# Forget-gate attention scores: two rounded passes over all 128 rows per head, in place of native fp32 over 64 rows

## The chip, the cores and the metric

The kernel runs on one core of one Trainium2 chip. The metric is the device time of one execution in microseconds (us). Engines are named as in the profile: PE is the matrix engine TensorE, PEld its weight loads, DVE is VectorE, ACT is ScalarE, SP issues transfers.

## The reference, cut to what matters

The program is two transformer layers and a third block over 512 tokens of width 1024. The change touches one place, the mixer of the second layer, attention with a forget gate, 16 heads of 64 channels (the function is cut):

```python
def _fox_attend(q, k, v, log_f):
    c = jnp.cumsum(log_f, axis=1)
    ...
        s = jnp.einsum('bqhd,bkhd->bhqk', q_b, k, preferred_element_type=jnp.float32) * (d ** -0.5)
        s = s + cq_b[..., :, None] - ck[:, :, None, :]
        s = jnp.where(kpos[None, :] <= qpos[:, None], s, NEG_INF)
        w = jax.nn.softmax(s, axis=-1).astype(v.dtype)
        return jnp.einsum('bhqk,bkhd->bqhd', w, v)
```

It runs for four blocks of 128 queries. Block number qb sees the keys of blocks 0 to qb, so its scores are 128, 256, 384 or 512 columns wide. `q`, `k` and `v` are projections of the layer's input.

## The kernel before

Every projection splits both operands into a rounded part (type fp32r, tiles with H) and the rest (tiles with L), and adds three products: high by high, low by high, high by low (L400, L401, L402 in `lin_parts`). A weight tile arrives by DMA in RAW, ACT rounds it to WH (`hi_ahead`, L364), DVE subtracts to get WL (`lo_ahead`, `lo_one`, L370), both three tiles ahead of use. ACT, DVE and PE each run a list that is fixed in the program and strictly in order; semaphores tie the lists together.

The forget-gate stage takes the 16 heads as 8 pairs. The two heads of a pair sit in one tile, one in rows 0 to 63, the other in rows 64 to 127. A pair is four steps, one per query block qb. In each step c of `pe_attend` PE issues

1. the scores of the next step (`pe_scores`, L483, native fp32; PE executes each such product as two records, so a step has four), and then the mask, a bf16 product per head added to the same bank (L491),
2. at qb = 0 the product of weights and values of the pair before (L529),
3. the transposes of this step's probabilities (L502),
4. `project_ahead`: six times three products (L400 to L402), a quarter of the 72 products that project queries (part 0), keys (part 1) and values (part 2) of the next pair. A part is eight times three products. Part 0 ends in the second call of step qb = 1, part 1 in the fourth call of step qb = 2; two more calls follow in that step, and then come the scores of the next pair's block 0, which need that pair's queries and keys.

ACT in a step copies the transposes out (L616) and computes the exponentials of the next step (L592); then in `project_ahead` it rounds one weight tile (L364) and copies one finished part out of its PSUM bank: QF (L2354) after qb = 1, KF (L2356) after qb = 2, VT (L2360) after qb = 3. DVE in a step adds the decay rows BC to the next step's scores and takes the row bound (L572), normalises (L605, L607), and then in `project_ahead` calls `skip()`, which subtracts one weight tile (L370) and does nothing else. The parts alternate between two PSUM banks; PE starts a part when the semaphore `evac` of its bank says that the one before was read.

ACC, 16 KB in each partition, isn't used during this stage.

Of the kernel before, what the change touches and what calls it, by code (L numbers as in the profile page):

```python
# [16 lines left out]
F32, F32R, BF16, I32 = mybir.dt.float32, mybir.dt.float32r, mybir.dt.bfloat16, mybir.dt.int32  # L17
ALU, ACT, AX = mybir.AluOpType, mybir.ActivationFunctionType, mybir.AxisListType
P = 128
T = 512  # L20
# [51 lines left out]
class Counts:  # L72
# [17 lines left out]
 ptev pv o_hi o_lo sinkexp bandv sum7 sum8 mean cen sqr var ln_t x_new h_relu h_sq h_hi h_lo fl fox_c chain_d  # L90
 chain_a chain_p out_t gate_t gate_s pt_hi pt_lo kept mem_in tabb_in sq2 rn r_hi r_lo pooled pw_in y_hi y_lo ix ixr ixs
 topk hsp hg_x hg_prod hg_read hg_e hg_d hg_o hg_small hx mn m2 varb ln_v x_full sum7q pj pj_free memsum cross xsum
 asum ysum h_up quad mvt yt yo ot_in xt_in z r_tok merge os brf var_out var_in""".split()


def program(nc, known, t):

    cnt = Counts(known)
    ctx = ExitStack()
    with ctx:  # L100
        sem = {n: ctx.enter_context(nc.semaphore(n)) for n in SEMS}
# [6 lines left out]
        evac = [ctx.enter_context(nc.semaphore(f"evac{b}")) for b in range(2)]  # L108
        PB = [ctx.enter_context(nc.psum_tensor(f"PB{i}", [P, T], F32)) for i in range(8)]
# [4 lines left out]
        def at(name, shape, dt, off):  # L114
            return nc.alloc_sbuf_tensor_at(name, shape, dt, offset=off)

        def sb(name, shape, dt):
            size = (int(np.prod(shape[1:])) * (2 if dt == BF16 else 4) + 31) // 32 * 32
            h = at(name, shape, dt, top[0])
            top[0] += size  # L120
            return h
# [8 lines left out]
        acc_at = top[0]  # L130
# [15 lines left out]
        def region(name, shape, dt):  # L146
            return sb(name, shape, dt)
# [7 lines left out]
        VT = region("VT", [P, T], F32)  # L155
# [40 lines left out]
        top[0] = mixer  # L196
        OH = region("OH", [P, DT, T], F32R)
        OL = region("OL", [P, DT, T], F32R)
        QF = region("QF", [P, 2, T], F32)
        KF = region("KF", [P, 2, T], F32)  # L200
        BC = region("BC", [P, 2, 2, T], F32)
        VP = region("VP", [P, 2, TT, P], F32)
        FZ = region("FZ", [16, 5, T], F32)
# [119 lines left out]
        def wait(eng, name, key):  # L323

            eng.wait_ge(sem[name], cnt.value(name, key))

        def done(ins, name, key):

            ins.then_inc(sem[name], 1)
            cnt.note(name, key)  # L330
# [13 lines left out]
        def evac_of(eng, m):  # L344

            eng.wait_ge(evac[m % 2], m // 2 + 1)
# [19 lines left out]
        def lo_one(eng, n):  # L366

            s, nb = n % 4, blocks_of(n)
            eng.wait_ge(hi_done[s], n // 4 + 1)
            eng.tensor_tensor(WL[:, s, 0:nb], RAW[:, s, 0:nb], WH[:, s, 0:nb].bitcast(F32), ALU.subtract).then_inc(lo_done[s], 1)  # L370

        def lo_ahead(dve, st, k=0, i=0, per=0):

            if per == 0:
                if st.n + k + 3 < total_tiles:
                    lo_one(dve, st.n + k + 3)
                return
            s, u = st.slot(k + 3, i, per)
            dve.wait_ge(hi_done[s], u + 1)
            dve.tensor_tensor(WL[:, s], RAW[:, s], WH[:, s].bitcast(F32), ALU.subtract).then_inc(lo_done[s], 1)  # L380
# [38 lines left out]
        def keys(kind, qb):  # L419

            return {"swa": list(range(max(qb - 1, 0), qb + 1)), "mem": [0, 1]}.get(kind, list(range(qb + 1)))
# [9 lines left out]
        def operands(kind, h):  # L431
            r = slice(h % 2 * 64, h % 2 * 64 + 64)
            if kind == "mla":
                return QM[:, h], KM[:, h], lambda j: V4[:, j, h * 64:h * 64 + 64]
            if kind == "swa":
                return QS[r, h // 2], K2[r, h // 4], lambda j: VS[:, j, h // 4 * 64:h // 4 * 64 + 64]
            if kind == "fox":
                pp = h // 2 % 2
                return QF[r, pp], KF[r, pp], lambda j: VP[:, pp, j, h % 2 * 64:h % 2 * 64 + 64]
            if kind == "dsa":  # L440
                return SQ_[r, h // 2], SK2[r], lambda j: SV[:, j]
            return MQ[r, h // 2], MK[r, h // 2], lambda j: MV[:, j, h * 64:h * 64 + 64]

        def item(kind, h, qb):

            return ((HEAD0[kind] + h) // 2 * 4 + qb) * 2 + h % 2
# [4 lines left out]
        def score_read(n):  # L451

            return "biased" if n // 8 in BIASED else "score_free"
# [5 lines left out]
        def pe_scores(pe, kind, g, qb):  # L459

            ns = [item(kind, 2 * g + e, qb) for e in range(2)]
            ks = keys(kind, qb)
            lo = (ks[0] - qb + 1) * P if kind == "swa" else 0
            w = len(ks) * P
            plain = kind in ("swa", "mem")
            xs = [None, None]
            for e in range(2):
                if ns[e] >= 2:
                    wait(pe, score_read(ns[e] - 2), ns[e] - 2)
            if kind == "fox" and qb == 0:  # L470
                evac_of(pe, M_FOX + 3 * g)
                evac_of(pe, M_FOX + 3 * g + 1)
            if kind == "swa" and qb == 0:
                evac_of(pe, M_A["q", g])
            if kind == "mla" and qb == 0:
                evac_of(pe, M_A["uq", 2 * g])
                evac_of(pe, M_A["uq", 2 * g + 1])
                evac_of(pe, M_A["ukv", 2 * g])
                evac_of(pe, M_A["ukv", 2 * g + 1])
                pe.wait_ge(sem["chain_a"], cnt.value("chain_a", "krope"))  # L480
            for e in range(2):
                q, k, _ = operands(kind, 2 * g + e)
                xs[e] = pe.matmul(PB[2 + e][:, lo:lo + w], q[:, qb * P:qb * P + P], k[:, ks[0] * P:ks[0] * P + w], start=True, stop=plain)  # L483
                if plain:
                    done(xs[e], "scores", ns[e])
            if not plain:
                for e in range(2):
                    if kind == "dsa":
                        x = pe.matmul(PB[2 + e][:, 0:w], ID16[:], MSK[:, qb, 0:w], start=False, stop=True)
                    else:  # L490
                        x = pe.matmul(PB[2 + e][:, w - P:w], ID16[:], CA16[:], start=False, stop=True)  # L491
                    done(x, "scores", ns[e])
# [391 lines left out]
        M_FOX = M_IN + 101  # L884
# [986 lines left out]
        def _(act):  # L1871
            st = Stream()
# [25 lines left out]
            def step():  # L1898
                hi_ahead(act, st)
                lin_ready(act, st)  # L1900

            def nxt():
                st.n += 1
                st.m += 1
# [444 lines left out]
            def project(j, part):  # L2349
                pp = j % 2  # L2350
                step()
                b, ub = st.bank(0)
                if part == 0:
                    x = act.activation(QF[:, pp], PB[b][:], ACT.Copy, scale=-0.125)  # L2354
                elif part == 1:
                    x = act.activation(KF[:, pp], PB[b][:], ACT.Copy)  # L2356
                else:
                    if j:
                        act.wait_ge(sem["misc"], cnt.value("misc", ("vp", j - 1)))
                    x = act.activation(VT[:], PB[b][:], ACT.Copy)  # L2360
                x.then_inc(evac[b], 1)
                nxt()
            for part in range(3):
                project(0, part)

            def project_ahead(c):
                j, qb = divmod(c, TT)
                if j < 7 and qb:
                    project(j + 1, qb - 1)
# [12 lines left out]
        def _(dve):  # L2382
            st = Stream()
# [24 lines left out]
            def nxt():  # L2408
                st.n += 1
                st.m += 1  # L2410

            def skip():
                lo_ahead(dve, st)
                nxt()
# [19 lines left out]
            def token_major(key, dst):  # L2434
                dve.wait_ge(sem["misc"], cnt.value("misc", key))
                done(dve.tensor_copy(dst, PB[7][:].rearrange("p (j n) -> p j n", n=P)), "misc_free", key)
# [722 lines left out]
            b, ub = st.bank(0)  # L3159
# [7 lines left out]
            done(dve.memset(FZ[:, 0], 1.0), "chain_d", "fone")  # L3167
            dve.wait_ge(sem["chain_d"], cnt.value("chain_d", "fone"))
            done(dve.tensor_tensor_scan(FZ[:, 3], FZ[:, 0], FZ[:, 2], 0.0, ALU.mult, ALU.add), "fox_c", 0)
            for part in range(3):  # L3170
                skip()
            token_major(("vp", 0), VP[:, 0])

            def project_ahead(c):
                j, qb = divmod(c, TT)
                if qb:
                    if j < 7:
                        skip()
                elif j:
                    token_major(("vp", j), VP[:, j % 2])  # L3180
            dve_attend(dve, ("fox",), 8, project_ahead)
            p_low(1)

# [43 lines left out]
```

## Time and profile before

| | |
|---|---|
| runs of the program | 2237.23, 2237.76, 2239.43 us; median 2237.76 |
| profiled execution, first to last instruction | 2236.6 us (the page shows no other time of it) |
| PE, PEld busy | 2182.0 us (98%), 1726.4 us (77%) |
| DVE, ACT, POOL busy | 1254.3 us (56%), 908.3 us (41%), 230.7 us (10%) |
| chain that ended last | PE 86%, DVE 8%, issue 3%, ACT 3% |
| forget-gate stage, first to last scores | 680.4 to 869.6 us |
| period of a pair | 25.37 us (725.60 to 750.97 us) |

The durations of matrix products overlap, since they are pipelined: what one costs is the distance between two starts. Before two products in a row the weights of the second are loaded under the first, where nothing hinders it. The busy times of PE count time spent in flight; they don't say that the engine is at its peak.

### The profile page before, as it was taken

The numbers are of one execution on the slowest core, as the hardware profiler recorded it, in microseconds if no ns is written. First come the engines' busy times: TensorE is split into PE (matmuls) and PEld (weight loads), VectorE is DVE, ScalarE is ACT, GpSimd is POOL, SyncE is SP. The second block draws the span as 40 slices with busy tenths as digits, with TensorE's granted clock in tenths as the row PEclk, the third lists the DMA queues.
The fourth block names the chain that finished last, engine by engine and source line by source line (L and its number), as shares of the span: only waits on it lengthen the run. The fifth ranks groups of instructions, "written<-read, shape, count | busy, mean of one in ns | idle before, by whom it ended". The sixth has DMA issues, their size and how long they took to land.

```text
span 2236.6 us, 27997 instructions
## 1 busy us (share of the span) xinstructions
PE 2182.0 (98%) x10187; PEld 1726.4 (77%) x10189; DVE 1254.3 (56%) x1993; ACT 908.3 (41%) x1502; POOL 230.7 (10%) x151
## 2 busy tenths in 40 slices
PE   7999999999999999999999999999999999999998
PEld 5767788888777777788888777678778787888886
DVE  5676643343474554643243377388589678544454
ACT  3565433233254544443243264433543444222333
POOL 0000400001400001400001320133000230000001
PEclk9999999999999999999999999999999999999999
DMA  6113233333223331333333244124222232323322
GB/s 173 27 45 102 74 98 104 86 102 103 76 77 100 98 95 48 94 94 106 92 94 103 78 112 110 56 72 113 73 66 66 75 105 76 103 76 113 94 68 73
DMA packets 368307, 196.92 MB, mean 88 GB/s; under 512 B 21040, under 2 KB 362813, under 8 KB 368206
## 3 DMA queue, kind: packets, MB, share of 16 engines
q1 hardware_dynamic: 367794, 195.51, 30.6%
q8 instruction: 63, 1.03, 0.2%
q14 instruction: 38, 0.31, 0.0%
q10 hardware_dynamic: 412, 0.07, 0.0%
HBM read 193.40 MB, written 2.14 MB: 87 GB/s over the span
## 4 chain that ended last, share of the span: by engine, by line
PE 86%; DVE 8%; issue 3%; ACT 3%; DMA 0%; POOL 0%; DVEq 0%; SPq 0%; ACTq 0%; POOLq 0%
PE PB L400 22%; PE PB L402 22%; PE PB L401 22%; PE PB L483 2%; PE PB L1392 2%; PE PB L1393 2%; PE PB L1394 2%; PE PB L529 2%; PE PB L502 2%; DVE ATT L2956 1%; PE PB L1279 1%; PE PB L1280 1%; PE PB L1283 1%; DVE WL L370 1%; PE PB L1378 0%
## 5 line engine op out<-in xcount | busy, mean ns | idle before, releaser
L364 ACT ACTIVATE WH<-RAW 128x1024 fp32r<-128x1024 f32 (+3 forms) x365 | 368.9, 1014 | 364.1 <-PE PB L402 343.1
L400 PE MATMUL PB<-XH,WH 128*128 128x512 f32 x1232 | 487.0, 395 | 5.1 <-DVE TG L3086 1.3
L402 PE MATMUL PB<-XH,WL 128*128 128x512 f32 x1232 | 480.2, 390 | 0.0
L401 PE MATMUL PB<-XL,WH 128*128 128x512 f32 x1232 | 479.6, 389 | 0.0
L380 DVE TENSOR_TENSOR WL<-RAW,WH 128x1024 fp32r<-128x1024 f32 x184 | 235.4, 1280 | 169.7 <-ACT WH L364 167.4
L400 PEld LDWEIGHTS PB<-XH,WH 128*128 128x128 f32 x1232 | 230.9, 187 | 59.2 <-issue 3.3
L402 PEld LDWEIGHTS PB<-XH,WL 128*128 128x128 f32 x1232 | 230.8, 187 | 49.5
L401 PEld LDWEIGHTS PB<-XL,WH 128*128 128x128 f32 x1232 | 231.1, 188 | 47.2 <-issue 0.7
L370 DVE TENSOR_TENSOR WL<-RAW,WH 128x1024 fp32r<-128x1024 f32 (+2 forms) x157 | 189.2, 1214 | 60.6 <-ACT WH L364 60.0
L400 PE MATMUL PB<-HH,WH 128*128 128x512 f32 x512 | 199.2, 389 | 0.0
L401 PE MATMUL PB<-HL,WH 128*128 128x512 f32 x512 | 199.2, 389 | 0.0
L402 PE MATMUL PB<-HH,WL 128*128 128x512 f32 x512 | 199.2, 389 | 0.0
L2574 DVE TENSOR_SCALAR HR<-PB 128x512 f32<-128x512 f32 x64 | 44.3, 691 | 144.8 <-PE PB L402 143.6
L1998 ACT ACTIVATE HS<-HR 128x512 f32<-128x512 f32 x64 | 40.5, 633 | 191.9 <-DVE HR L2574 191.9
L616 ACT ACTIVATE PT<-PB 128x256 f32<-128x256 f32 (+3 forms) x160 | 65.5, 412 | 124.2 <-PE PB L502 124.1
L776 POOL TENSOR_TENSOR SM<-ACC 128x512 f32<-128x512 f32 x4 | 5.2, 1294 | 1061.7 <-DVE ACC L2560 570.2
L400 PEld LDWEIGHTS PB<-HH,WH 128*128 128x128 f32 x512 | 96.1, 188 | 20.1
L402 PEld LDWEIGHTS PB<-HH,WL 128*128 128x128 f32 x512 | 96.1, 188 | 19.9
L401 PEld LDWEIGHTS PB<-HL,WH 128*128 128x128 f32 x512 | 96.1, 188 | 19.8
L1392 PE MATMUL PB<-XH,WH 128*128 128x512 f32 x256 | 102.9, 402 | 0.4 <-ACT RS L2112 0.4
L1394 PE MATMUL PB<-XH,WL 128*128 128x512 f32 x256 | 99.8, 390 | 0.0
L1393 PE MATMUL PB<-XL,WH 128*128 128x512 f32 x256 | 99.8, 390 | 0.0
(520 smaller groups left out, 3570.7 us busy)
## 6 DMA issues: line engine op xcount, KB each, us to landing
RAW<-in_w_up SPq DMA_DIRECT2D x64, 512.0 KB, 4.0
RAW<-in_w_down SPq DMA_DIRECT2D x64, 512.0 KB, 3.6
RAW<-in_w_ffn_gate_up SPq DMA_DIRECT2D x44, 512.0 KB, 3.8
RAW<-in_w_gate SPq DMA_DIRECT2D x32, 512.0 KB, 4.0
RAW<-in_od_w_in SPq DMA_DIRECT2D x24, 512.0 KB, 6.4
RAW<-in_w_in SPq DMA_DIRECT2D x24, 512.0 KB, 4.0
RAW<-in_ple_w_gate SPq DMA_DIRECT2D x16, 512.0 KB, 3.7
RAW<-in_w_ffn_down SPq DMA_DIRECT2D x16, 512.0 KB, 3.9
```

The lines of the kernel that those rows point to most:

```text
L364: act.activation(WH[:, s, 0:nb], RAW[:, s, 0:nb], ACT.Copy).then_inc(hi_done[s], 1)
L370: eng.tensor_tensor(WL[:, s, 0:nb], RAW[:, s, 0:nb], WH[:, s, 0:nb].bitcast(F32), ALU.subtract).then_inc(lo_done[s], 1)
L380: dve.tensor_tensor(WL[:, s], RAW[:, s], WH[:, s].bitcast(F32), ALU.subtract).then_inc(lo_done[s], 1)
L400: pe.matmul(PB[b][0:m, 0:n], WH[:, s, k, 0:m], rh[:, kk, :], start=kk == 0, stop=False)
L401: pe.matmul(PB[b][0:m, 0:n], WH[:, s, k, 0:m], rl[:, kk, :], start=False, stop=False)
L402: x = pe.matmul(PB[b][0:m, 0:n], WL[:, s, k, 0:m], rh[:, kk, :], start=False, stop=kk == last)
L483: xs[e] = pe.matmul(PB[2 + e][:, lo:lo + w], q[:, qb * P:qb * P + P], k[:, ks[0] * P:ks[0] * P + w], start=True, stop=plain)
L502: x = pe.transpose(PB[4 + e][:, c * P:c * P + P], PR[:, e, c * P:c * P + P], ID[:])
L616: done(act.activation(PT[:, e, ks[0]:ks[0] + len(ks), qb * P:qb * P + P], PB[4 + e][:, 0:len(ks) * P].rearrange("p (j q) -> p j q", q=P), ...
L1392: pe.matmul(PB[m % 2][:], WH[:, n % 4, k], XH[:, k], start=k == 0, stop=False)
L1393: pe.matmul(PB[m % 2][:], WH[:, n % 4, k], XL[:, k], start=False, stop=False)
L1394: x = pe.matmul(PB[m % 2][:], WL[:, n % 4, k], XH[:, k], start=False, stop=k == DT - 1)
```

## The change

The scores' operands become rounded parts and rests, stacked over all 128 rows. For head e of a pair, QTWO holds the rounded queries in the head's own 64 rows and the rest in the other 64 rows. KHIGH holds the rounded keys in both halves, KLOW the rest of the keys in both halves. One product of QTWO with KHIGH, over 128 rows, gives rounded by rounded plus rest by rounded; the second, QTWO with KLOW, adds the products with the keys' rest. So a step has four fp32r products over 128 rows (two per head) where it had four records over 64 rows. QTWO and KHIGH lie in ACC, KLOW where QF and KF were.

```diff
 def pe_scores
-                evac_of(pe, M_FOX + 3 * g + 1)
+                pe.wait_ge(sem["k_hi"], cnt.value("k_hi", (g, "twice", 1)))
+                pe.wait_ge(sem["k_lo"], cnt.value("k_lo", (g, 1)))
...
+                if kind == "fox":
+                    for part, keys_of in enumerate(k):
+                        pe.matmul(PB[2 + e][:, 0:w], q[:, qb * P:qb * P + P], keys_of[:, 0:w], start=part == 0, stop=False)
+                    continue
 ACT, def project
-                    x = act.activation(QF[:, pp], PB[b][:], ACT.Copy, scale=-0.125)
+                    for e in range(2):
+                        r = slice(e * 64, e * 64 + 64)
+                        done(act.activation(QTWO[r, pp, e], PB[b][r], ACT.Copy, scale=-0.125), "q_hi", (j, e))
                 elif part == 1:
-                    x = act.activation(KF[:, pp], PB[b][:], ACT.Copy)
+                    for e in range(2):
+                        r = slice(e * 64, e * 64 + 64)
+                        done(act.activation(KHIGH[r, pp, e], PB[b][r], ACT.Copy), "k_hi", (j, e))
+                    for e in range(2):
+                        r, other = slice(e * 64, e * 64 + 64), slice((1 - e) * 64, (1 - e) * 64 + 64)
+                        act.wait_ge(sem["k_hi"], cnt.value("k_hi", (j, e)))
+                        done(act.activation(KHIGH[other, pp, e], KHIGH[r, pp, e].bitcast(F32), ACT.Copy), "k_hi", (j, "twice", e))
 DVE, in place of skip(), for parts 0, 1 and 2 of every pair
+            def fox_lows(j, part):
+                lo_ahead(dve, st)
+                b, ub = st.bank(0)
+                pp = j % 2
+                if part == 0:
+                    dve.wait_ge(sem["q_hi"], cnt.value("q_hi", (j, 1)))
+                    for e in range(2):
+                        r, into = slice(e * 64, e * 64 + 64), slice((1 - e) * 64, (1 - e) * 64 + 64)
+                        x = dve.scalar_tensor_tensor(QTWO[into, pp, e], PB[b][r], -0.125, QTWO[r, pp, e].bitcast(F32), ALU.mult, ALU.subtract)
+                    x.then_inc(evac[b], 1)
+                elif part == 1:
+                    dve.wait_ge(sem["k_hi"], cnt.value("k_hi", (j, 1)))
+                    for e in range(2):
+                        r = slice(e * 64, e * 64 + 64)
+                        x = dve.tensor_tensor(KLOW[r, pp, e], PB[b][r], KHIGH[r, pp, e].bitcast(F32), ALU.subtract)
+                    x.then_inc(evac[b], 1)
+                    dve.wait_ge(evac[b], ub + 1)
+                    for e in range(2):
+                        r, other = slice(e * 64, e * 64 + 64), slice((1 - e) * 64, (1 - e) * 64 + 64)
+                        done(dve.tensor_copy(KLOW[other, pp, e], KLOW[r, pp, e]), "k_lo", (j, e))
+                nxt()
```

## Rows read from the trace of the kernel before

**Rows 1.** Window: length, busy us (instructions) of PE, PEld, DVE, ACT, POOL; clock; DMA share, GB/s.

```profile
704.00:728.00 24.00, 24.00 (x132) 17.12 (x131) 12.25 (x35) 11.15 (x29) 0.00 (x0) 1.00 0.26 74
```

**Rows 2.** Timeline of PE, 718 to 732 us: start, duration (us), engine, line, operation.

```profile
718.57 0.39 PE L402 MATMUL PB<-OH,WL 128*128 128x512 f32 x1
...
719.25 0.39 PE L402 MATMUL PB<-OH,WL 128*128 128x512 f32 x1
719.56 1.13 PE L483 MATMUL PB<-KF,QF 64*128 64x512 f32 x4
720.63 0.29 PE L491 MATMUL PB<-CA,ID 128*128 128x128 bf16 x2
...
725.60 0.49 PE L483 MATMUL PB<-KF,QF 64*128 64x128 f32 x4
726.02 0.28 PE L491 MATMUL PB<-CA,ID 128*128 128x128 bf16 x2
...
730.91 0.39 PE L402 MATMUL PB<-OH,WL 128*128 128x512 f32 x1
...
731.87 0.29 PE L491 MATMUL PB<-CA,ID 128*128 128x128 bf16 x2
```

**Rows 3.** Timeline of PE in the third block, products of 256 columns.

```profile
1343.38 0.28 PE L1330 MATMUL PB<-MH,WH 128*128 128x256 f32 x1
...
1343.61 0.28 PE L1332 MATMUL PB<-MH,WL 128*128 128x256 f32 x1
```

**Rows 4.** Timeline of all engines around one pair's keys, and the next pair's scores.

```profile
723.59 1.05 ACT L364 ACTIVATE WH<-RAW 128x1024 fp32r<-128x1024 f32 x1
...
724.54 0.58 ACT L2356 ACTIVATE KF<-PB 128x512 f32<-128x512 f32 x1
...
724.68 1.23 DVE L370 TENSOR_TENSOR WL<-RAW,WH 128x1024 fp32r<-128x1024 f32 x1 [0.27 <-ACT WH L364]
...
750.97 0.49 PE L483 MATMUL PB<-KF,QF 64*128 64x128 f32 x4
```

**Rows 5.** Groups by form: count, busy us, mean ns of one, idle before them.

```profile
L636 DVE TENSOR_TENSOR XL<-PB,XH 128x512 fp32r<-128x512 f32 x7 | 4.8, 692 | 14.6 <-ACT XH L629 14.6
...
L1925 ACT ACTIVATE KM<-KR 64x512 f32<-64x512 f32 x8 | 4.5, 617 | 0.1
...
L2466 DVE COPY RTQ<-KR 32x512 f32<-32x512 f32 x1 | 0.4, 422 | 0.0
```

**Rows 6.** Timeline of all engines around one pair's queries.

```profile
718.27 0.58 ACT L2354 ACTIVATE QF<-PB 128x512 f32<-128x512 f32 x1
...
718.40 1.23 DVE L370 TENSOR_TENSOR WL<-RAW,WH 128x1024 fp32r<-128x1024 f32 x1 [0.34 <-ACT WH L364]
...
721.00 0.69 DVE L572 CUSTOM_DVE_ANT_0 SW<-PB,BC 128x512 f32<-128x512 f32 x1 [1.38 <-PE PB L491]
...
721.62 0.69 DVE L572 CUSTOM_DVE_ANT_0 SW<-PB,BC 128x512 f32<-128x512 f32 x1
```

**Rows 7.** Timeline where scores waited for DVE, start of the stage.

```profile
681.60 0.08 DVE L572 DVE_READ_ACCUMULATOR2_ANT STAT<- 128x1 f32 x1
681.80 0.33 PEld L483 LDWEIGHTS PB<-KF,QF 64*128 64x128 f32 x4 [0.88 <-DVE STAT L572]
```

**Rows 8.** Timeline of PE after three long waits; then windows: length, busy, clock, DMA.

```profile
250.68 0.47 PE L1279 MATMUL PB<-XH,WH 128*128 128x512 f32 x1 [1.86 <-ACT XH L764]
...
926.04 0.47 PE L1279 MATMUL PB<-XH,WH 128*128 128x512 f32 x1 [1.75 <-ACT XH L764]
...
1738.20 2.02 PE L1486 MATMUL PB<-XX 128*128 128x128 f32 x16 [2.26 <-DVE ATT L2956]
...
252.00:254.00 2.00, 2.00 (x7) 0.52 0.00 0
254.00:256.00 2.00, 2.00 (x7) 0.62 0.00 0
...
682.00:684.00 2.00, 2.00 (x10) 0.54 0.04 13
```

More of the change, by code:

```diff
@@ L92 @@
  topk hsp hg_x hg_prod hg_read hg_e hg_d hg_o hg_small hx mn m2 varb ln_v x_full sum7q pj pj_free memsum cross xsum
- asum ysum h_up quad mvt yt yo ot_in xt_in z r_tok merge os brf var_out var_in""".split()
+ asum ysum h_up quad mvt yt yo ot_in xt_in z r_tok merge os brf var_out var_in q_hi k_hi k_lo""".split()
 def program(nc, known, t):
@@ L198, in program @@
         OL = region("OL", [P, DT, T], F32R)
-        QF = region("QF", [P, 2, T], F32)
-        KF = region("KF", [P, 2, T], F32)
+        KLOW = region("KLOW", [P, 2, 2, T], F32R)
+        QTWO = at("QTWO", [P, 2, 2, T], F32R, acc_at)
+        KHIGH = at("KHIGH", [P, 2, 2, T], F32R, acc_at + 8192)
         BC = region("BC", [P, 2, 2, T], F32)
@@ L438, in operands @@
                 pp = h // 2 % 2
-                return QF[r, pp], KF[r, pp], lambda j: VP[:, pp, j, h % 2 * 64:h % 2 * 64 + 64]
+                return QTWO[:, pp, h % 2], (KHIGH[:, pp, h % 2], KLOW[:, pp, h % 2]), lambda j: VP[:, pp, j, h % 2 * 64:h % 2 * 64 + 64]
             if kind == "dsa":
@@ L2359, in project @@
                         act.wait_ge(sem["misc"], cnt.value("misc", ("vp", j - 1)))
-                    x = act.activation(VT[:], PB[b][:], ACT.Copy)
-                x.then_inc(evac[b], 1)
+                    act.activation(VT[:], PB[b][:], ACT.Copy).then_inc(evac[b], 1)
                 nxt()
@@ L3169, in _ @@
             done(dve.tensor_tensor_scan(FZ[:, 3], FZ[:, 0], FZ[:, 2], 0.0, ALU.mult, ALU.add), "fox_c", 0)
+            def fox_lows(j, part):
[19 more added lines that the diff above has]
+                nxt()
             for part in range(3):
-                skip()
+                fox_lows(0, part)
             token_major(("vp", 0), VP[:, 0])
@@ L3177, in project_ahead @@
                     if j < 7:
-                        skip()
+                        fox_lows(j + 1, qb - 1)
                 elif j:
```

## The prediction, made before the changed kernel was timed

> **What bounds the kernel now.** I read the page first: PE has 98% of the span and 86% of the chain that ended last, so time that PE wins or loses in this stage moves the end. The windows of 24 us over the forget-gate stage say the same: PE is never out of work, the clock is full (1.00, 2.4 GHz), DVE is busy 12.25 us of 24 and ACT 11.15 [rows 1]. PE does not wait for the other two in the steady part of the stage. That doesn't make them harmless: the question is how early they are with what PE needs next. So I read next the timeline of PE around the scores, for what the edit removes and adds there [rows 2, 3]; then the timeline of all engines between the end of a pair's key projection and that pair's first scores [rows 4], because this is where the added work must be finished; then the same around the queries [rows 6]. It is the second of these that decides.
>
> **PE, the products.** All costs are distances between starts. Products of 512 columns follow each other by 0.227 us (three distances from 718.57 to 719.25 [rows 2]). Before, the scores of 512 columns with what lies around them take from 719.25 (start of the last projection product) to 720.63 (start of the mask): 1.38 us. Of this 0.31 lies ahead of the first score record (719.25 to 719.56), 0.08 more than the usual distance: the 64-row records start late after 128-row ones; another such gap lies ahead of the mask. After, five distances of ordinary 128-row products take the place of it: 5 x 0.227 = 1.14 us, a gain of 0.24. At 256 columns it was 730.91 to 731.87, 0.96 us. fp32r products of 256 columns follow by 0.12 us (two distances in 0.23 [rows 3]), so after it is 0.23 + 4 x 0.12 = 0.71, a gain of 0.25. At 384 columns I take the same 0.25, since both neighbours give it. At 128 columns no row of an fp32r product exists. Low bound: the weight loads pace it, at most the 0.12 of the 256-column row, 4 x 0.12 = 0.48 us against 0.42 now (725.60 to 726.02 [rows 2]); high bound: a narrow fp32r product costs per column what a head's fp32 records do, (1.07 - 0.42) / 384 = 1.7 ns [rows 2], so 0.22 us each, 0.87 in all. The nearer row is that of 256 columns, so I take 0.06 lost for each pair; the high bound would lose 0.45, or 3.6 us over 8 pairs.
>
> There is a price that could be missed here: the two heads of a pair lie in different rows, and their records ran side by side; 128-row products can't. Present score times are 0.42 us at 128 columns and 1.07 at 512 [rows 2], 0.745 on average; doubled, they would add 8 x 4 x 0.745 = 23.8 us. The rows don't bear that out, since four fp32r products of 512 columns take 4 x 0.227 = 0.91 us, less than four fp32 records side by side. The Trainium skill, TensorEngine Tiling (Array Packing), section Performance Considerations, speaks against the change here: a contraction of 64 rows is to be row-tiled by two, for up to twice the speed. By that rule the sum would get up to 23.8 us more in place of PE's gain; the measured distances of both types in this trace say otherwise, since the rule compares products of one type.
>
> Which of these gains reach the end? 256 and 384 columns: 8 x 0.50 = 4.0 us. The gain at 512 columns is spent, in seven of eight pairs, on reaching the wait below sooner, because that wait is paced by the list of DVE: it counts once, 0.25. At 128 columns 8 x 0.06 = 0.5 lost. PE's gain is 3.8 us.
>
> **ACT and DVE, the operands.** For each pair ACT's one copy of QF becomes two of 64 rows, its one of KF becomes four. The duration goes by columns, not rows: a 64x512 copy takes 617 ns, the 128x512 one of the queries 580 [rows 5, 6]. That is 4 x 0.6 = 2.4 us more ACT per pair. DVE gets two subtractions for the queries, two for the keys, at the 692 ns of such a one from PSUM, and two copies between rows at 422 ns [rows 5], 3.6 us per pair. In a period of 25.37 us both have room. What matters is the place.
>
> *Queries.* They are finished in step qb = 1 and needed a step and a half later. ACT's two copies end at 718.27 + 1.1 = 719.4, DVE's weight subtraction at 719.63, then two subtractions until about 720.95; DVE's next work, the row bound of 512 columns, starts at 721.00 [rows 6]. It fits exactly. PE would now be 0.24 us earlier with those scores, so DVE becomes their limit there: that is why the gain at 512 columns is lost.
>
> *Keys.* Here nothing fits. ACT starts the copy at 724.54, bound by its own weight tile (723.59 + 1.05 [rows 4]), and is done at 725.12; PE starts the next pair's scores at 725.60. So there is half a microsecond of slack, and the new list is:
> - ACT: rounded keys, head 0 and head 1, then both copied to the other rows. Its instructions overlap by 0.1 (724.64 to 724.54 [rows 4]), so the first two are done about 725.65 and the last about 726.7.
> - DVE: the weight subtraction stands ahead in its list, from 724.68 for 1.23 us, to 725.91 [rows 4]. The rests of the keys start then, 0.61 us apart (721.00 to 721.62 for rows of this size [rows 6]), the second ends at 727.15. DVE waits for its own result, about 0.1 us. Two copies of 0.42, overlapping by 0.07, end at 728.0.
> - PE is awake 0.12 us after the instruction it waits for ended (681.60 + 0.08 to 681.80 [rows 7]): 728.14 in place of 725.60.
>
> So the scores start 2.5 us later, and nothing on PE hides it: its list is in order, and behind this wait stand the mask, the transposes and the values' projection. Bounds: if the copies between rows of an fp32r tile cost a subtraction's 0.69 us, 0.5 us more; if DVE's part were done sooner and ACT's four copies set the time, 726.7 + 0.12, a delay of 1.2 us. For the first pair the values' projection of 5.4 us lies between keys and scores and hides all. The seven others run on one pattern (725.60 and, a period later, 750.97 [rows 2, 4]): 7 x 2.5 = 17.5 us, bounds 8.4 and 21.
>
> Nothing further is late: DVE is idle for half of each window [rows 1]; the bank of the queries is read by 721.0, and PE writes it again with the values' projection from about 724.1 on, two calls or 1.4 us ahead of the scores at 725.60; DMA and SP keep their order, with the transfer engines busy 0.26 of the time [rows 1].
>
> **The clock.** PE's idle time at each of these waits is 2.5 plus what it arrives early, about 2.8 us. Three waits of 1.75 to 2.26 us stand in the trace [rows 8]. After the first the granted clock fell to its lower level, 1.2 GHz: 0.52 and 0.62 in two windows of 2 us, (0.48 + 0.38) x 2 = 1.7 us lost. After the others it did not. At the start of this stage it fell too, to 0.54 in 682 to 684 us, after two waits close together. So two of four cases, from shorter waits than ours. With seven waits of 2.8 us I take three falls, 3 x 1.7 = 5.1 us; bounds 0 and 12.
>
> **Sum.** -3.8 + 17.5 + 5.1 = +18.8 us on the span of 2236.6, so 2255.4. The median of the runs lies 1.2 above the span: 2256.6.
>
> **Rivals.**
> - *The same wait, no fall of the clock*: +13.7, 2251.5. The two waits without a fall [rows 8] speak for it, that ours are longer against it.
> - *All dear*: a fall at nearly each wait (12), narrow fp32r products at 0.22 us (3 more) or dear copies: +26 to +35, 2264 to 2273.
> - *ACT's four copies set the wait, DVE is done sooner*: 7 x 1.2 - 3.8 = +4.6, 2242.4. DVE's own list speaks against it: its first new instruction can't start ahead of 725.9, and four must follow.
> - *The heads' lost overlap doubles the score time*: +17.5 + 23.8 + 5.1 = +46, 2284. A product of 512 columns would have to stand 0.5 us from the next; it stands 0.227 [rows 2]. This is the rule of the skill's page on tiling, above.
> - *Faster*: the rests of the keys are ready when PE comes, so that only the products' gain stays, with the one at 512 columns: -5.5, 2232. The place is the wait ahead of the next pair's first scores. It decides below 3.8 / 7 = 0.54 us of delay per pair; the list above has 2.5. Only if the trace's order of DVE and ACT were not the program's could this be.
>
> **How the numbers follow.** Chances: the forecast with one to five falls 0.56, no fall 0.15, all dear 0.17, ACT sets it 0.06, doubled scores 0.02, faster 0.04. The likeliest gives 2257 (2253 to 2261 by itself). The range goes from the no-fall case with a somewhat shorter wait, 2247, into the dear cases, 2267. A change of 0.2% is 4.5 us, about what a measurement of this kernel can tell from none: faster 0.04, same 0.03, slower 0.93.
>
> **What would show it.** Right: the first load of L483's 128-column group waits seven times for DVE's copy into KLOW, 2.7 to 3.0 us each; the pair's period is about 27.3 us without a fall of the clock and 29 with one; scores to mask take 0.9 us at 512 columns; outside 680 to 870 us nothing moves. Wrong: if the wait names ACT's KHIGH instead, if the period stays near 25, if the clock stays at 1.00 throughout or falls in each pair, or if products of 128 columns stand more than 0.12 us apart.

## The result, and the profile after

The changed kernel takes 2270.72 us (median of 4 runs, 2267.89 to 2273.30) against 2237.49 us before: 1.0143 times as long, 95% interval [1.0131, 1.0155]. It is slower by 33 us. The range forecast ended at 2267.

The page of the kernel after, its first parts:

```profile
span 2266.1 us, 28077 instructions
...
PE 2190.8 (97%) x10187; PEld 1748.9 (77%) x10189; DVE 1282.3 (57%) x2041; ACT 927.7 (41%) x1534; POOL 230.6 (10%) x151
...
PEclk9999999999999998999999999999999999999999
```

ACT and DVE have only 19 and 28 us more to do. PE's busy time grew by 9 us of the 29.5 by which the span grew, though it has as many instructions (10187) as before; the other 20.7 us PE does nothing. So the waits of PE between 676 and 925 us come next (what it waited for: total us, times, longest):

```profile
PE PB L487 <- DVE KLOW L3203: 20.3, 7, 2.9
PE PB L487 <- DVE STAT L578: 0.8, 1, 0.8
```

Seven waits of 2.9 us, each for DVE's copy into KLOW, the instruction that the prediction named. The timeline of all engines around one pair's keys, after (it answers to [rows 4]):

```profile
725.66 1.05 ACT L365 ACTIVATE WH<-RAW 128x1024 fp32r<-128x1024 f32 x1
...
726.61 1.19 ACT L2366 ACTIVATE KHIGH<-PB 64x512 fp32r<-64x512 f32 x2
726.74 1.23 DVE L371 TENSOR_TENSOR WL<-RAW,WH 128x1024 fp32r<-128x1024 f32 x1 [0.27 <-ACT WH L365]
...
727.03 0.39 PE L403 MATMUL PB<-OH,WL 128*128 128x512 f32 x1
727.71 1.27 ACT L2370 ACTIVATE KHIGH<-KHIGH 64x512 fp32r<-64x512 f32 x2
727.88 1.38 DVE L3198 TENSOR_TENSOR KLOW<-PB,KHIGH 64x512 fp32r<-64x512 f32 x2
729.30 0.87 DVE L3203 CAST KLOW<-KLOW 64x512 fp32r<-64x512 f32 x2
730.32 0.30 PE L487 MATMUL PB<-KHIGH,QTWO 128*128 128x128 f32 x1 [2.90 <-DVE KLOW L3203]
730.46 0.27 PE L487 MATMUL PB<-KLOW,QTWO 128*128 128x128 f32 x1
...
730.79 0.28 PE L497 MATMUL PB<-CA,ID 128*128 128x128 bf16 x2
```

The reader sees the list work itself off: ACT's weight tile, four copies in two rows, DVE's weight subtraction, two rests, two copies; PE's last projection product starts at 727.03 and the next at 730.32. The products became cheaper as computed. PE around the scores of 384 and 512 columns, after ([rows 2] has the 512 before):

```profile
715.87 0.39 PE L403 MATMUL PB<-OH,WL 128*128 128x512 f32 x1
716.10 0.33 PE L487 MATMUL PB<-KHIGH,QTWO 128*128 128x384 f32 x1
...
716.80 0.28 PE L497 MATMUL PB<-CA,ID 128*128 128x128 bf16 x2
...
721.23 0.39 PE L403 MATMUL PB<-OH,WL 128*128 128x512 f32 x1
721.46 0.39 PE L487 MATMUL PB<-KHIGH,QTWO 128*128 128x512 f32 x1
...
722.37 0.28 PE L497 MATMUL PB<-CA,ID 128*128 128x128 bf16 x2
```

From the last projection product to the mask it is 1.14 us at 512 columns (1.38 before) and 0.93 at 384. What cost more than forecast is the clock, which the profile gives as a share of 2.4 GHz; a fall is a stretch at 0.50, 1.2 GHz. Windows of 2 us around two of the seven waits (length, busy us and count of PE, granted clock, DMA share, GB/s):

```profile
728.00:730.00 2.00, 0.00 (x0) 1.00 1.05 309
730.00:732.00 2.00, 1.68 (x15) 1.00 1.15 294
732.00:734.00 2.00, 2.00 (x10) 1.00 0.64 170
...
816.00:818.00 2.00, 0.11 (x1) 0.86 1.11 324
818.00:820.00 2.00, 2.00 (x11) 0.50 1.20 290
820.00:822.00 2.00, 2.00 (x8) 0.50 0.44 117
822.00:824.00 2.00, 2.00 (x6) 0.50 0.00 0
824.00:826.00 2.00, 2.00 (x9) 0.93 0.00 0
```

Behind the wait that ended at 730.32 the clock stayed at 2.4 GHz. Ahead of the end of the one at 817.89 it fell to 1.2 GHz and stayed there until 824: (0.14 + 0.50 x 3 + 0.07) x 2 = 3.4 us of clock missing, twice the price of the fall before [rows 8]; 3.2 of them while PE worked. It fell at six of the seven waits. I added (1 - clock) x length over windows of 0.25 us in which PE worked throughout: 16.0 us in the stage after, 1.7 before. The stage, first scores to last, went from 189.2 us (680.38 to 869.62) to 219.3 us (679.76 to 899.07): +30.1, of which the clock is 14.3 and all the rest 15.8. Outside, next to nothing moved: the stage begins 0.6 us earlier, and from the last scores to the end of the span it is 1367.0 us in both.

### The profile page after: what moved, and what is told of

Same layout as the page of the kernel before. It is cut to its first block, busy times and chain, and to the rows that moved or that the text cites. A ratio compares the mean times of both kernels' runs of the same rounds, so it can differ in the third digit from the quotient of the medians.

```text
span 2266.1 us, 28077 instructions
## 1 busy us (share of the span) xinstructions
PE 2190.8 (97%) x10187; PEld 1748.9 (77%) x10189; DVE 1282.3 (57%) x2041; ACT 927.7 (41%) x1534; POOL 230.6 (10%) x151
## 3 DMA queue, kind: packets, MB, share of 16 engines
q1 hardware_dynamic: 367794, 195.51, 30.1%
## 4 chain that ended last, share of the span: by engine, by line
PE 51%; DVE 6%; issue 2%; ACT 2%; DVEq 0%; ACTq 0%
PE PB L401 13%; PE PB L403 13%; PE PB L402 13%; PE PB L1398 2%; PE PB L1400 2%; PE PB L1399 2%; DVE ATT L2969 1%; PE PB L535 0%; PE PB L1285 0%; DVE WL L371 0%; PE PB L1384 0%; PE PB L1386 0%; PE PB L1385 0%; PE PB L1286 0%; PE PB L1289 0%
```

## The experiments

Ten experiments in four groups. Each was timed beside the kernel before, whose median was 2237.4 to 2238.5 us. All compute what the reference does, but for one, as said there.

**Where the loss is.** Later scores on PE, with ACT's and DVE's lists untouched:

```diff
 pe_attend
+                late = kind == "fox" and qb == TT - 1 and c + 1 < len(steps)
-                if c + 1 < len(steps):
+                if c + 1 < len(steps) and not late:
                     pe_scores(pe, *steps[c + 1])
 ...
                 pe_transposes(pe, kind, g, qb)
-                between(c)
+                if late:
+                    between(c, 0, 4)
+                    pe_scores(pe, *steps[c + 1])
+                    between(c, 4, 6)
+                else:
+                    between(c)
```

> The changed kernel; PE alone issues the scores of the next pair's block 0 later: after the transposes of step qb = 3 and four of its six projection calls (3.5 us later). ACT's and DVE's lists stay. Theory (the wait for the keys' rests, with the fall of the clock behind it, is the whole loss): no wait of L487's group for KLOW, clock at 1.00 in the stage, and the products' gain stays, with 512 columns in all pairs: 2237.5 - 6 = 2231.5 us (2229 to 2234). Rival (ACT's and DVE's added work, or the place of the operands, slows the stage by itself): above 2245 us with PE waiting elsewhere.

Measured: 2233.28 us, 0.9980 [0.9970, 0.9989]. No wait for KLOW is left, the clock is at 1.00 all through the stage. So all of the loss hangs on that one wait; the added instructions on ACT and DVE and the place of the operands cost nothing that shows beside it. The control:

> Control: the kernel before with the same later issue of those scores. Both theories: 2237.5 us, within 1.5, since nothing waits there. If the order by itself gains or costs something, it shows here and is to be taken off the run with the changed kernel.

The same edit on the kernel before: 2239.68 us, 1.0009 [0.9999, 1.0019], not told apart from no change, though 2.2 us above the other median, where the expectation allowed 1.5. In its profile a pair takes 25.46 us (753.49 to 778.95) against 25.37: a second switch from other products to the projection's, at 0.09 us, 0.6 us over the stage. The two profiled spans differ by 2.0 us. Of the other 1.4, 0.9 lie at the very end, where the clock fell at 2226.9 us, with PE still at work on its last products (before, it fell at 2228.4, behind them), and 0.4 ahead of the stage. The other falls are two in each profile, at 252 and 682 us before and at 681 and 1739 here, each behind waits that all kernels have, so they cancel. With the new products under the same order a pair takes 24.60 us (726.89 to 751.49): 0.86 us less, 6.9 us for eight pairs, and 6.4 by the medians.

**The clock by itself.** Unused products fill PE's wait, so that the scores start when they did and only PE's idle time changes. Twelve, four and, later, eight of them:

```diff
 pe_scores, kind == "fox" and qb == 0
+                for _ in range(12 if g else 0):
+                    pe.matmul(PB[2][:], OH[:, 0, 0:P], OL[:, 0, :], start=True, stop=True)
                 pe.wait_ge(sem["k_hi"], cnt.value("k_hi", (g, "twice", 1)))
                 pe.wait_ge(sem["k_lo"], cnt.value("k_lo", (g, 1)))
```

> The changed kernel with 12 products of 512 columns that nobody reads, ahead of PE's wait for the keys, in pairs 1 to 7 (12 x 0.227 = 2.7 us of work inside a wait of 2.9 us). Theory (falls of the clock because PE idles make 15 us of the loss): the clock stays at 1.00 in the stage, the scores start when they did, 2237.5 + 17.8 - 3.8 - 1.7 = 2250 us (2247 to 2253). Rival (the low clock has another cause, such as the kind of products): 2270 us, low clock as before.

> The changed kernel with four unused products of 512 columns (0.9 us) ahead of the wait for the keys, in place of twelve. The scores start when they did, but PE idles 2.0 us instead of 2.9. Theory (how often and how long the clock falls goes by the length of the idle time): between the filled run (2255.4 us, no fall at these waits) and the changed kernel (2270.7): two or three falls of 1.7 us, 2259 us (2255 to 2264). Rival (a stop of any such length costs the clock the same): 2270 us.

> The changed kernel with eight unused products of 512 columns ahead of the wait for the keys (1.8 us), so that PE idles 1.1 us at an unchanged start of the scores. Theory (idle time decides over the clock): none or one fall at these waits, 2253.5 us (2252 to 2256). Rival (each stop has its own chance to cost the clock, whatever its length): as with four products, 2258 us.

Measured: 2255.40 us with twelve, 2257.99 with four, 2256.35 with eight. The waits of the one with eight, and its timeline at one of them:

```profile
PE PB L489 <- DVE KLOW L3205: 7.7, 7, 1.1
```

```profile
753.95 0.39 PE L403 MATMUL PB<-OH,WL 128*128 128x512 f32 x1
754.18 1.98 PE L474 MATMUL PB<-OL,OH 128*128 128x512 f32 x8
757.26 0.30 PE L489 MATMUL PB<-KHIGH,QTWO 128*128 128x128 f32 x1 [1.11 <-DVE KLOW L3205]
```

A kernel that does more work is faster by 14 us: PE is merely kept from idling, and the low clock at these waits is gone. The three kernels start their scores at the same distance of 27.66 us per pair (729.60 to 757.26 with eight, 730.54 to 758.21 with twelve, 790.55 to 818.21 with four, where the clock didn't fall), as does the changed kernel where it didn't (730.32 to 757.98). The one with twelve came out 5.4 us above its expectation, and its profile accounts for that. Without the clock its stage takes 203.4 us where the kernel before takes 187.5, 15.9 more, and the expectation had 14.0; the clock fell once in the third block (0.52 in a window at 1754 us, at a wait that all kernels have), 1.7 us, and once at the start of the stage, 1.7 us, where the expectation had none. That makes 5.3. The one with eight also lies above what was expected, 2253.5 (2252 to 2256); its stage without the clock takes 203.9 us, and it too has the fall at 1754.

**The length of the wait.** Shorter, by leaving out DVE's rests of the keys (KLOW is set to zero once, so the products with the keys' rests add zeros: this part of the computation is left out), and shorter by order alone:

> The changed kernel without DVE's work on the keys' rests: KLOW is zeroed once and PE waits for ACT's four copies alone. Left out: the products with the keys' rests are products with zeros. Theory (DVE's list ends the wait, the length of the wait decides over the clock): the wait is named ACT KHIGH, about 1.75 us instead of 2.9 us, seven times; 17.8 - 8 = 10 us of delay, and the clock falls in two to four of seven, once each: 2249 us (2246 to 2253). Rival (any wait at this place costs the clock as much as the long ones did): 10 - 4 + 15, 2259 us. Rival (ACT's copies set the wait anyway): 2270 us.

```diff
 ACT, project, part 1, pairs 1 to 7: the weight tile (hi_ahead) behind the four copies of the keys
 DVE, fox_lows, part 1, pairs 1 to 7: the weight tile (lo_ahead) behind rests and copies, and
-                    dve.wait_ge(sem["k_hi"], cnt.value("k_hi", (j, 1)))
                     for e in range(2):
+                        dve.wait_ge(sem["k_hi"], cnt.value("k_hi", (j, e)))
                         r = slice(e * 64, e * 64 + 64)
```

> The changed kernel; in pairs 1 to 7 ACT and DVE handle the keys ahead of their weight tile, and DVE starts on head 0 when ACT's first copy is done. PE's order stays. Theory (the wait is the length of these lists): ACT no longer waits for its weight tile (0.5 us sooner), DVE starts its rests 1.2 us sooner, PE's wait falls from 2.9 to about 1.7 us; delay 17.8 - 8 = 10 us, clock 2 to 7 us: 2249 us (2246 to 2254). Rival (the weight tiles, late by 2 us, hold PE up elsewhere): no better than 2265 us with waits for WL. Rival (ACT's copies alone set the wait): the same wait of 1.85 us as without the rests.

Longer, by making DVE's two copies twice:

> The changed kernel with DVE's two copies of the keys' rests made twice in each pair, so that the wait grows by about 0.85 us, to 3.75 us. Theory (idle time decides over the clock): 7 x 0.85 = 6 us of delay, and the clock falls at each of the seven waits for 3.4 us of loss, 24 us in place of 15: 2270.7 + 6 + 8 = 2285 us (2279 to 2288). Rival (the clock's loss doesn't grow any more): 2277 us.

And the changed kernel once more:

> The changed kernel once more, unaltered, for a second profile and more runs beside the others. Theory (waits are fixed by the lists, the clock falls anew in each execution): seven waits for KLOW of 2.9 us as before, within 0.1 us; falls of the clock at five to seven of them, not the same pairs; 2267 to 2273 us. Rival (the clock falls at fixed places of the program): the same six pairs with the same losses.

Measured: 2253.22 us without the rests, 2250.98 with the keys first, 2273.38 with the longer list, 2270.82 for the repetition. PE's waits in the four, in this order:

```profile
PE PB L487 <- ACT KHIGH L2377: 12.8, 7, 1.9
```

```profile
PE PB L487 <- DVE KLOW L3209: 12.2, 7, 1.8
```

```profile
PE PB L487 <- DVE KLOW L3207: 26.7, 7, 3.8
```

```profile
PE PB L487 <- DVE KLOW L3203: 20.4, 7, 2.9
```

The waits have the lengths of the lists. Without the rests ACT's copies end the wait, at 1.8 us. From the row bound of 512 columns to the scores it is then 6.17 us (749.12 to 755.29), 1.57 more than before, where the prediction put ACT's bound at 1.2. Its median lies 0.2 us above the range expected (2246 to 2253). All together, from one profiled execution each (the loss again over windows of 0.25 us in which PE worked throughout, behind the seven waits alone):

| PE idle at each wait | kernel | falls at 7 waits | lost to the clock, us | that execution, us | median, us |
|---|---|---|---|---|---|
| 0.2 us | twelve products | 0 | 0 | 2255.95 | 2255.40 |
| 1.1 | eight products | 0 | 0 | 2255.15 | 2256.35 |
| 1.75 | keys first | 2 | 3.4 | 2248.21 | 2250.98 |
| 1.8 | no rests | 2 | 3.4 | 2250.53 | 2253.22 |
| 2.0 | four products | 3 | 5.1 | 2260.61 | 2257.99 |
| 2.9 | changed | 6 | 16.0 | 2267.89 | 2270.72 |
| 2.9 | changed, again | 7 | 18.9 | 2271.04 | 2270.82 |
| 3.8 | longer list | 7 | 16.4 | 2274.44 | 2273.38 |

The falls belong to the profiled execution and not to the median. With the keys first, and without the rests, it was the fastest of four, with four products the slowest; by the times, and the mean clocks (0.996 in that execution with the keys first, 0.994 in the other three), the others of the first two had more falls, at these waits or elsewhere, and those of the third fewer. So the counts from 1.75 to 2.0 us say a few in seven and no order among these three.

Two steps: how often the clock falls grows with the idle time at these waits, and from 2.9 us on a fall costs more, because then it mostly begins well inside the wait and lasts twice as long. Which pairs it hits is not fixed: in the repetition the second wait had a fall, in the first profile it had none.

The longer list missed both expectations, 2285 and 2277. All seven waits have a fall, but part of the low clock now lies in the idle time, where it costs nothing. Windows of that kernel around one wait, which ended at 794.11:

```profile
792.00:794.00 2.00, 0.00 (x0) 0.68 1.17 326
794.00:796.00 2.00, 1.89 (x10) 0.50 1.11 272
796.00:798.00 2.00, 2.00 (x9) 0.50 0.12 36
798.00:800.00 2.00, 2.00 (x7) 0.61 0.00 0
```

Of 3.4 us of missing clock, 0.6 lie before 794, while PE waits. The profiles bear the rest out: against the repetition, 6.3 us more wait, 2.5 less lost behind the waits, and falls elsewhere that differ by one each way, are +3.8; the spans differ by 3.4.

**A version that beats both.** The keys first on ACT and DVE as above, and on PE three projection calls ahead of the scores, with the transposes kept right behind them:

```diff
 pe_attend
+                late = kind == "fox" and qb == TT - 1 and c + 1 < len(steps)
+                if late:
+                    between(c, 0, 3)
                 if c + 1 < len(steps):
                     pe_scores(pe, *steps[c + 1])
 ...
                 pe_transposes(pe, kind, g, qb)
-                between(c)
+                if late:
+                    between(c, 3, 6)
+                else:
+                    between(c)
```

> The lists of the run with the keys first, and on PE three of the six projection calls of step qb = 3 (2.04 us) ahead of the next pair's scores, the transposes still right behind these scores. Theory: the three calls cover a wait of 1.7 us, and the mask is again followed by the transposes, so that the extra change of operand type that the run with later scores paid (2 us over seven pairs, by the control) is gone: 2231.3 us (2229.5 to 2233). Rival (the transposes, 2 us later, make the values of that pair wait for ACT's copies): waits for PT of up to 0.5 us in each pair, 2234 to 2235 us.

Measured: 2230.84 us (8 runs), 0.9972 [0.9961, 0.9982]. The time is the expected one, but not for the whole reason given: a pair takes 24.51 us (699.96 to 724.46), 0.09 less than with the scores alone moved, so the second switch was worth 0.6 us over the stage and not 2. The difference of 2.4 us between the two medians is more than that; falls of the clock, which each execution has at other places, are of this size (251 and 1733 us in the profile with the scores alone moved, 680 us alone in this one). The timeline, all engines:

```profile
723.31 0.88 DVE L3215 CAST KLOW<-KLOW 64x512 fp32r<-64x512 f32 x2
723.67 1.06 ACT L365 ACTIVATE WH<-RAW 128x1024 fp32r<-128x1024 f32 x1
724.46 0.22 PE L487 MATMUL PB<-KHIGH,QTWO 128*128 128x128 f32 x1
...
724.99 1.04 PE L508 MATMUL PB<-ID,PR 128*128 128x128 f32 x8
```

The copy ends at 724.19, and PE starts at 724.46, 0.22 us behind the product before it and without a wait in its row. But the load of its weights starts at 724.30, 0.11 us behind the copy's end and 0.06 behind the start of the product before it, where with the scores alone moved it starts together with that product (726.66). So the keys come just in time; next to no slack is left.

## Why the prediction was wrong, point by point

- *PE, the products: right.* Forecast 1.14 us at 512 columns, 0.71 at 256, 0.48 at 128 and a gain of 0.25 at 384; measured 1.14, 0.70 (735.69 to 736.39), 0.47 (730.32 to 730.79) and a gain of 0.24 (0.93 against 1.17, 713.63 to 714.80 before). The case that no row showed, an fp32r product of 128 columns, is paced at 0.11 us, so the high bound and the doubled price for the lost overlap are both refuted. The gain with no wait in the way was put at 5.5 us and is 6.4 to 6.9.
- *Queries: right, with a little over.* DVE's row bound of 512 columns starts 1.84 us behind the last projection product (721.23 to 723.07), 1.75 before [rows 2, 6]. So DVE's queries made it late by 0.1 us, where the forecast had it just fit.
- *Keys, the wait: right in place, cause, count and nearly in size.* From that row bound to the scores it took 4.60 us before (721.00 to 725.60) and takes 7.25 (723.07 to 730.32): 2.65 later where 2.54 was forecast. A pair without a fall of the clock takes 27.66 us, where 27.3 was forecast. Everything but the clock made +15.8 us in the stage; the forecast had +13.7.
- *The clock: the step that failed.* That the clock would fall behind these waits was right; the term was mis-sized. "With seven waits of 2.8 us I take three falls, 3 x 1.7 = 5.1 us." There were six, in a second execution seven, and four or five of them cost 3.1 to 3.2 us of working time and not 1.7. Net of the fall that the stage had before, this is 14.3 us where 5.1 stood (which counted no fall before). The count was taken from waits of 1.75 to 2.26 us, two falls in four, and carried over to waits of 2.8 us, though the text itself noted that ours were longer. (Its rows also left out a wait of 2.19 us at 129.59 us, behind which the clock did not fall: two falls in five.) The runs with 1.75 to 2.0 us show about that share, two or three in seven, and those with 2.9 us nearly all. The price was taken from falls that began once PE was at work again. The bound of 12 us had the same flaw: it multiplied seven falls by the short price. Of the 14.1 us between the forecast 2256.6 and the median 2270.72, the clock's term makes 9.2 and the delay 2.1; the other 2.8 are the distance from the profiled execution, the fastest of four, to the median.
- *The rivals.* "All dear" came closest, 2264 to 2273, by its first part alone, nearly a fall at each wait, and even that part had 12 us where 14.3 net came; its other parts, dear narrow products and dear copies (422 ns measured, 422 forecast), did not happen. So its range meeting the result is in part luck. Its own terms, 13.7 + 12 + 3 + 3.5, also add up to 32 and not to 35. "ACT's four copies set the wait" wasn't this kernel's case: with the copies of ACT alone PE waits 1.8 us, here 2.9 for DVE. The faster case exists, but only with another order on PE.
- What stays open: what decides at which of several equal waits the clock falls.

## What to carry to other kernels

Before operands get a longer preparation, measure the slack of the instruction that needs them first, not the idle share of the engines that prepare them; here 0.5 us of slack stood against half-idle ACT and DVE. A repeated stop of a matrix engine costs more than its length: price it by rows of stops as long as its own, and ask whether the clock would fall while the engine still waits. If such a stop can't be moved behind other work, even useless products in it can pay, here 14 of the 33 us.

## What the runs showed of the hardware that was not expected

- At the seven waits for the keys, in one profiled execution of each kernel, the granted clock never fell with idle times of 0.2 and 1.1 us (14 waits); at 1.75 to 2.0 us it fell at 7 of 21, at 2.9 us at 13 of 14, at 3.8 us at 7 of 7.
- Length alone doesn't decide. Four other waits stand in all twelve profiled executions: near 250 us (1.9 us long) the clock fell in nine of them, near 130 us (2.2 to 2.4 us) in two, near 1740 us (2.3 us) in four, near 930 us (1.75 us) in none. At the start of the stage, where two waits of 0.7 to 0.8 us end 2 us apart, it fell in six.
- At the waits for the keys a fall took 1.7 us of clock when it began less than 0.1 us ahead of PE's restart, or behind it, and 3.4 us when it began 0.4 us or more ahead; nothing between was seen. Of the 3.4 us, 3.1 to 3.2 fell on PE's work at waits of 2.9 us, 2.5 to 2.9 at 3.8 us.
- The same seven waits gave different falls in two executions. The runs of this kernel spread by 5.4 us (2267.89 to 2273.30), and their mean granted clock goes from 0.990 in the fastest to 0.988 in the slowest.
